# First mixer's probabilities transposed on VectorE and over DRAM instead of on TensorE

## The chip, the cores and the metric

The kernel runs on one core of a Trainium2 chip. The metric is the device time of one execution in microseconds (us). Engines are called by the profile's names: PE is TensorE (PEld its weight loads), DVE is VectorE, ACT is ScalarE, POOL is GpSimd, SP is SyncE. A name like L1737 is line 1737 of the kernel.

## The reference, cut to what matters

A decoder trunk of two layers on 512 tokens of width 1024. Layer 0 mixes tokens with three groups of dilated attention (16 heads of width 64), layer 1 with differential attention; each layer has a squared-ReLU MLP and a gated embedding behind the mixer. Only layer 0's mixer is changed:

```python
qkv = (h @ w_qkv).reshape(B, T, N_GROUPS_A, 3, HEADS_A, HEAD_DIM)
for g, (window, dilation) in enumerate(DIL_CONFIGS):      # (128,1), (512,4), (2048,16)
    o, l = dilated_group_attention(qkv[:, :, g, 0], qkv[:, :, g, 1], qkv[:, :, g, 2],
                                   window, dilation, rel_table)
    ...
alpha = softmax(stack(lses), axis=0)
o = sum(alpha[..., None] * stack(outs), axis=0)
return o.reshape(B, T, D_MODEL) @ w_o
```

Within a group: scores of queries against keys, plus a bias, a softmax over the keys, and the probabilities times the values. The last product contracts over the keys, and the scores have the queries on the partitions, so the probabilities are transposed in between.

## The kernel before

**Units.** Every weight matrix is cut into units of 1024x128. SP loads one (512 KB) into `w_raw` (L679), ACT rounds it to `w_hi` (`split_hi`, L884), DVE subtracts to get `w_lo` (`split_lo`, L1196), and PE multiplies in 24 matmuls of 512 columns (hi*hi, hi*lo, lo*hi; L1661 to L1663, or L1825 to L1827 where values are the rows). There are two buffers for each of these tiles. SP may issue the load of unit u once DVE has made `w_lo` of unit u-2.

**Steps and slots of the first mixer.** Heads go in pairs. Step s runs in nine slots, one unit each (the q, k, v projections of pair s), and beside them the attention of pair s-1. Steps 1 to 7 have both; step 8, the drain, has no projection and runs the first output units instead. On every engine `sub_a` writes out what slot i does, in the order of the program; for PE the attention's work of a slot stands ahead of the slot's unit. Odd steps make the far groups' values of two pairs in slots 0 to 3 (`values_unit`, evacuated together in slot 3); even steps have nine ordinary units.

**The attention of a pair** has four items (`ph` 0 and 1: the near group, 2 and 3: the two far groups), each a tile `probs[ph]` of 128x1024 in fp32:

- `scores_a` on PE into the bank `logits` (even items) or `turned` (odd items): items 0 and 1 in slot 0, items 2 and 3 in slot 2.
- Bias and row minimum on DVE (L1299, four instructions an item) and the exponential on ACT (L992), item i in slot i.
- The merge of the three groups' sums: `far_ps` on PE (L1848) and a chain of small DVE and ACT operations in slot 4, `near_ps` (L1857) in slot 6.
- `scale_a` on DVE (L1284, four instructions an item): items 2, 3, 0, 1 in slots 4, 5, 6, 7.
- `turn` on PE (L1737): 128x128 transposes of items 2 and 3 ahead of slot 6's unit (16 of them), of items 0 and 1 behind slot 8's unit (14), each bank copied back over `probs[ph]` half by ACT (L978, L1006) and half by DVE (L1305, L1368).
- `values_a` on PE (L1806) at the end of slot 8 into `attn`, which ACT and DVE split into the operand of the output projection (L1011, L1372).

SP's queue holds more than weights: `load_bias_a` in slot 3, `expand_a` in slot 6 (steps 1 to 6; ten DRAM to DRAM copies in small pieces that spread the next pair's bias, L711 and L715), and pieces of the second mixer's bias (L738) in slots 0, 4 and 8. SP counts its slots by the unit that it loads, some three slots ahead of PE. POOL does set-up and then waits for the first norm's sums (L866), behind the first mixer.

Of the kernel before, what the change touches and what calls it, by code (L numbers as in the profile page):

```python
# [65 lines left out]
A_SCORES = range(A_ITEMS)  # L66
A_MERGE = A_ITEMS
A_SCALES = {4: 2, 5: 3, 6: 0, 7: 1}
A_TURNS = {6: (2, 3), 8: (0, 1)}
A_NEAR = min(A_TURNS)  # L70
DRAIN_TURNS = {6: (2, 3), 7: (0, 1)}
DRAIN_SCALES = {4: (2,), 5: (3,), 6: (0, 1)}
A_TURN_ORDER = [ph for at_slot in sorted(A_TURNS) for ph in A_TURNS[at_slot]]
# [169 lines left out]
def build(nc, x, p, rel_bias, a_w_qkv, a_w_o, b_w_qkv, b_w_o, lq1, lk1, lq2, lk2, subln, norm_mix,  # L243
          norm_mlp, w_ff1, w_ff2, norm_ple, w_gate, w_proj, final_norm, selector, out):
    ctx = ExitStack()
    with ctx:
# [29 lines left out]
        probs_t = sb("probs_t", [P, T])  # L276
        ple_hi = [sb(f"ple_hi{i}", [P, KP, T], F32R) for i in range(2)]
# [64 lines left out]

        unit_out = [ps(f"unit_out{i}", [P, T]) for i in range(2)]
# [6 lines left out]
        near_in = attn[:, 0:2 * NT]  # L350
# [43 lines left out]
        def turns_at(has_proj, i):  # L394

            return (A_TURNS if has_proj else DRAIN_TURNS).get(i, ())

        def turns_behind(has_proj, i):

            return has_proj and i == A_UNITS - 1  # L400
# [181 lines left out]
        probs_ready = sem("probs_ready")  # L582
        turned_ready = sem("turned_ready")
# [233 lines left out]
        def _(pool):  # L817
# [43 lines left out]

            for norm in range(1, 7):
# [8 lines left out]
        def _(sc):  # L871
# [96 lines left out]
            def sub_a(s, par, i, has_proj, has_attn):  # L968
# [34 lines left out]
                if has_attn and turns_behind(has_proj, i):  # L1003
                    for ph in turns_at(has_proj, i):
                        wait(sc, turned_ready, (s - 1).times(A_ITEMS) + (A_TURN_ORDER.index(ph) + 1))
                        sc.activation(probs[ph][:, 0:T], a_bank(ph)[:, 0:T], ACT.Copy  # L1006
                                      ).then_inc(pt_a_ready, 1)
# [90 lines left out]
            def sub_b(s, par, i, has_proj, has_scores, has_prev, has_norm):  # L1098
# [6 lines left out]
                if has_prev:  # L1105
                    keys = b_width((i - 1) % B_ITEMS)
                    wait(sc, turned_ready, t)
# [81 lines left out]
        def _(ve):  # L1189
# [100 lines left out]
            def sub_a(s, par, i, has_proj, has_attn):  # L1290
                u = s.times(A_UNITS) + i
                start = s.reg is None and s.const == 0 and i == 0
                if has_attn and i in A_SCORES:
                    if i == 0:
                        wait(ve, bias_ready[1 - par], ((s - 1).half() + 1).times(16 * BIAS_LOADS))
                    wait_apart(ve, scores_ready, (s - 1).times(A_ITEMS) + (i + 1), (s_small, 16 * SMALL))
                    for cols, low_col, _ in a_segments(i):
                        to, of, by = probs[i][:, cols], a_bank(i)[:, cols], a_bias(1 - par, i, cols)
# [3 lines left out]
                if has_attn and not turns_behind(has_proj, i):  # L1302
                    for ph in turns_at(has_proj, i):
                        wait(ve, turned_ready, (s - 1).times(A_ITEMS) + (A_TURN_ORDER.index(ph) + 1))
# [11 lines left out]
                if has_attn and i == A_MERGE:  # L1316
# [14 lines left out]
                if has_attn and i == A_MERGE:  # L1331
# [17 lines left out]
                if has_attn and i == A_NEAR:  # L1349
# [783 lines left out]
```

## Time and profile before

| | |
|---|---|
| runs | 1615.31, 1614.57, 1614.43 us (median 1614.57) |
| profiled execution: span | 1614.3 us |
| PE busy | 1599.0 us (99%), 8244 matmuls |
| PEld, DVE, ACT, POOL busy | 82%, 56%, 38%, 4% |
| granted PE clock, mean | 0.998 |
| first mixer's steps 2 to 7 | 60.94 us each |
| DMA | 160.12 MB, mean 99 GB/s |

The profiled execution has no time of its own beside its span of 1614.3 us; the median of the runs lies 0.3 us above it, and that is taken for what lies around the span. A matmul's own duration in the profile is longer than the distance to the next one, since matmuls overlap: distances between starts say what PE work costs.

### The profile page before, as it was taken

The numbers are of one execution on the slowest core, as the hardware profiler recorded it, in microseconds if no ns is written. First come the engines' busy times: TensorE is split into PE (matmuls) and PEld (weight loads), VectorE is DVE, ScalarE is ACT, GpSimd is POOL, SyncE is SP. The second block draws the span as 40 slices with busy tenths as digits, with TensorE's granted clock in tenths as the row PEclk, the third lists the DMA queues.
The fourth block names the chain that finished last, engine by engine and source line by source line (L and its number), as shares of the span: only waits on it lengthen the run. The fifth ranks groups of instructions, "written<-read, shape, count | busy, mean of one in ns | idle before, by whom it ended". The sixth has DMA issues, their size and how long they took to land.

```text
span 1614.3 us, 22075 instructions
## 1 busy us (share of the span) xinstructions
PE 1599.0 (99%) x8244; PEld 1320.5 (82%) x8244; DVE 907.1 (56%) x1585; ACT 608.3 (38%) x1092; POOL 65.8 (4%) x68
## 2 busy tenths in 40 slices
PE   9999999999999999999999999999999999999998
PEld 7788888888888788888888878888878888888887
DVE  5365455555555863635455676777675363535565
ACT  5234334334334431222223444766652222222344
POOL 1000000000000200000001110000020000000111
PEclk9999999999999999999999999999999999999999
DMA  5633433443332333333333333323233333333331
GB/s 163 156 111 94 116 116 91 115 118 84 99 89 69 105 91 98 96 95 93 101 91 104 99 108 95 92 78 94 63 92 102 94 91 104 91 104 91 92 113 70
DMA packets 300571, 160.12 MB, mean 99 GB/s; under 512 B 31545, under 2 KB 295282, under 8 KB 300514
## 3 DMA queue, kind: packets, MB, share of 16 engines
q1 hardware_dynamic: 300112, 158.61, 34.6%
q0 software_dynamic: 144, 0.71, 0.2%
q8 instruction: 37, 0.61, 0.2%
q14 instruction: 20, 0.16, 0.0%
q10 hardware_dynamic: 258, 0.04, 0.0%
HBM read 157.11 MB, written 10.60 MB: 104 GB/s over the span
## 4 chain that ended last, share of the span: by engine, by line
PE 95%; POOL 1%; DMA 1%; DVE 1%; ACT 1%; issue 0%; SPq 0%; POOLq 0%; ACTq 0%; DVEq 0%
PE unit_out L1661 26%; PE unit_out L1663 26%; PE unit_out L1662 25%; PE turned L1737 2%; PE attn L1806 2%; POOL sumsq L866 1%; PE attn L2060 1%; PE unit_out L1825 1%; PE logits L1737 1%; DMA w_raw<-in_a_w_qkv_dram 1%; PE unit_out L1827 1%; PE unit_out L1826 1%; PE logits L1661 1%; PE misc L1737 1%; PE misc L1661 1%; PE misc L1663 1%
## 5 line engine op out<-in xcount | busy, mean ns | idle before, releaser
L1661 PE MATMUL unit_out<-act_hi,w_hi 128*128 128x512 f32 x1849 | 725.9, 393 | 3.0 <-DVE w_lo L1196 1.7
L1663 PE MATMUL unit_out<-act_hi,w_lo 128*128 128x512 f32 x1849 | 718.8, 389 | 0.0
L1662 PE MATMUL unit_out<-act_lo,w_hi 128*128 128x512 f32 x1849 | 718.0, 388 | 0.0
L884 ACT ACTIVATE w_hi<-w_raw 128x1024 fp32r<-128x1024 f32 (+3 forms) x256 | 271.0, 1058 | 461.2 <-PE unit_out L1663 349.4
L1661 PEld LDWEIGHTS unit_out<-act_hi,w_hi 128*128 128x128 f32 x1849 | 347.2, 188 | 78.2 <-DVE w_lo L1196 4.4
L1663 PEld LDWEIGHTS unit_out<-act_hi,w_lo 128*128 128x128 f32 x1849 | 347.1, 188 | 72.8
L1662 PEld LDWEIGHTS unit_out<-act_lo,w_hi 128*128 128x128 f32 x1849 | 347.4, 188 | 69.6 <-issue 0.2
L1196 DVE TENSOR_TENSOR w_lo<-w_raw,w_hi 128x1024 fp32r<-128x1024 f32 (+3 forms) x256 | 320.2, 1251 | 121.7 <-ACT w_hi L884 121.6
L1058 ACT ACTIVATE act_hi<-hidden 128x512 fp32r<-128x512 f32 x64 | 40.5, 633 | 243.4 <-DVE hidden L1459 243.4
L866 POOL TENSOR_TENSOR sumsq<-sumsq,square 128x512 f32<-128x512 f32 x41 | 57.8, 1410 | 1525.2 <-ACT square L912 1523.5
L1456 DVE TENSOR_TENSOR scaled<-unit_out,rstd 128x512 f32<-128x512 f32 x62 | 42.8, 690 | 67.8 <-PE unit_out L1663 67.7
L1275 DVE TENSOR_TENSOR h_a<-h_a,unit_out 128x512 f32<-128x512 f32 x39 | 26.8, 687 | 90.0 <-PE unit_out L1663 90.0
L1275 DVE TENSOR_TENSOR heads<-heads,unit_out 128x512 f32<-128x512 f32 x40 | 27.5, 686 | 84.2 <-PE unit_out L1663 84.2
L992 ACT ACTIVATE probs<-probs,w_raw 128x256 f32<-128x256 f32 (+1 forms) x128 | 61.8, 484 | 32.4 <-DVE w_raw L1299 32.4
L1462 DVE TENSOR_TENSOR act_lo<-hidden,act_hi 128x512 fp32r<-128x512 f32 x64 | 44.3, 692 | 44.7 <-ACT act_hi L1058 44.7
L1459 DVE SCALAR_TENSOR_TENSOR hidden<-scaled 128x512 f32<-128x512 f32 x64 | 44.3, 692 | 2.2
L1540 DVE CUSTOM_DVE_ANT_0 probs<-logits,bias 128x512 f32<-128x512 f32 (+3 forms) x64 | 28.2, 486 | 26.0 <-PE logits L1663 26.0
L1114 ACT ACTIVATE probs<-probs,low 128x512 f32<-128x512 f32 (+3 forms) x64 | 35.4, 554 | 7.4 <-DVE low L1540 7.4
L899 ACT ACTIVATE act_hi<-heads,gains 128x512 fp32r<-128x512 f32 x24 | 17.3, 722 | 49.1 <-DVE heads L1275 25.6
L1284 DVE TENSOR_SCALAR probs<-probs,w_raw 128x256 f32<-128x256 f32 (+1 forms) x128 | 35.2, 339 | 0.3
L1299 DVE CUSTOM_DVE_ANT_0 probs<-logits,bias 128x256 f32<-128x256 f32 (+1 forms) x64 | 21.1, 386 | 20.4 <-PE logits L1788 20.4
L1737 PE MATMUL turned<-ident,probs 128*128 128x128 f32 x208 | 30.5, 279 | 0.0
(295 smaller groups left out, 1390.9 us busy)
## 6 DMA issues: line engine op xcount, KB each, us to landing
w_raw<-in_w_ff_dram SPq DMA_DIRECT2D x128, 512.0 KB, 4.0
w_raw<-in_a_w_qkv_dram SPq DMA_DIRECT2D x56, 512.0 KB, 3.9
w_raw<-in_b_w_qkv_dram SPq DMA_DIRECT2D x24, 512.0 KB, 5.1
w_raw<-in_a_w_qkv_dram SPq DMA_DIRECT2D x32, 256.0 KB, 3.0
w_raw<-in_w_ple_gate_dram SPq DMA_DIRECT2D x16, 512.0 KB, 4.0
bias_tiles_b<-bias_vectors SPq DMA_DIRECT2D x16, 256.0 KB, 4.5
bias<-bias_tiles_b SPq DMA_DIRECT2D x8, 512.0 KB, 3.9
w_raw<-in_a_w_o_dram SPq DMA_DIRECT2D x8, 448.0 KB, 3.6
```

Source lines behind the costliest of these rows:

```text
L866: pool.tensor_tensor(sumsq[:, :], sumsq[:, :], square[n % 2][:, :], ALU.add).then_inc(sumsq_done, 1)
L884: sc.activation(weights_of(u)[0][:, 0:width, :], w_raw[par][:, 0:width, :], ACT.Copy).then_inc(hi_done, 1)
L992: e = sc.activation(probs[i][:, cols], probs[i][:, cols], ACT.Exp, bias=low_col, scale=-1.0, accum_out=sum_col)
L1196: ve.tensor_tensor(lo[:, 0:width, :], w_raw[par][:, 0:width, :], hi[:, 0:width, :], ALU.subtract).then_inc(lo_done, 1)
L1275: ve.tensor_tensor(h[:, n, :], h[:, n, :], unit_out[u.const % 2][:, :], ALU.add).then_inc(evac_done, 1)
L1456: ve.tensor_tensor(scaled[:, :], bank_of(u)[:, :], rstd[:, :], ALU.mult).then_inc(evac_done, 1)
L1459: ve.scalar_tensor_tensor(hidden[:, :], scaled[:, :], 0.0, scaled[:, :], ALU.max, ALU.mult).then_inc(hid_ready, 1)
L1462: ve.tensor_tensor(MID[layer][1][:, n, :], hidden[:, :], MID[layer][0][:, n, :], ALU.subtract).then_inc(hid_done, 1)
L1661: te.matmul(bank, w_k[0], hi, start=start, stop=False)
L1662: te.matmul(bank, w_k[0], lo, start=False, stop=False)
L1663: return te.matmul(bank, w_k[1], hi, start=False, stop=stop)
L1737: last = te.transpose(bank[:, dst:dst + P], src, ident[:, :])
```

## The change

In steps 1 to 7 PE transposes no probabilities any more. For each item:

1. DVE transposes the 32x32 blocks of `probs[ph]` into a new tile `blocks[:, ph, :]` (one instruction over 128x1024; slots 3, 4, 5, 6 for items 2, 3, 0, 1).
2. POOL's queue stores that tile to DRAM (512 KB), waits until it has landed, and loads it back into `probs[ph]` in four DMAs of 32 partitions (128 KB each, in runs of 1 KB), which puts the blocks in their places.
3. `values_a` waits for the four loads and reads `probs[ph]` in runs of 32 columns (`turned_order`).

In the same steps the scores of items 2 and 3 move from slot 2 to slot 1, additions and exponentials of items 0, 1 to slot 0 and of 2, 3 to slot 1, the merge from slots 4 and 6 to slots 2 and 4, scaling to slots 2 to 5; the near sums go through the bank `turned` instead of `attn`. The copies back (ACT and DVE) are gone in these steps. The drain keeps its slots, its transposes and its copies. `blocks` lies over `ple_hi`/`ple_lo`, which are filled after the mixer. The computation is the same.

```diff
-A_SCORES = range(A_ITEMS)
-A_MERGE = A_ITEMS
-A_SCALES = {4: 2, 5: 3, 6: 0, 7: 1}
-A_TURNS = {6: (2, 3), 8: (0, 1)}
-A_NEAR = min(A_TURNS)
+A_TURN_ORDER = (2, 3, 0, 1)
+
+A_SCORES = {0: (0, 1), 1: (2, 3)}
+A_SOFT = {0: (0, 1), 1: (2, 3)}
+A_SPREAD, A_MERGE, A_NEAR = 1, 2, 4
+A_SCALES = {2: (2,), 3: (3,), 4: (0,), 5: (1,)}
+A_BLOCKS = {3: (2,), 4: (3,), 5: (0,), 6: (1,)}
+
+DRAIN_SCORES = {0: (0, 1), 2: (2, 3)}
+DRAIN_SOFT = {n: (n,) for n in range(A_ITEMS)}
+DRAIN_SPREAD, DRAIN_MERGE, DRAIN_NEAR = 3, 4, 6
+DRAIN_SCALES = {4: (2,), 5: (3,), 6: (0, 1)}
 DRAIN_TURNS = {6: (2, 3), 7: (0, 1)}
...
+        with nc.sbuf_tensor("blocks", [P, A_ITEMS, 2 * T], F32) as blocks:
+            pass
...
+        blocks_d = nc.dram_tensor("turned_blocks", (A_ITEMS, P, 2 * T), F32, kind="Internal")
...
-        near_in = attn[:, 0:2 * NT]
...
+        def near_in(has_proj):
+
+            return (turned if has_proj else attn)[:, 0:2 * NT]
...
+        def blocks_at(has_proj, i):
+
+            return A_BLOCKS.get(i, ()) if has_proj else ()
...
+        def merge_slots(has_proj):
+
+            return (A_SPREAD, A_MERGE, A_NEAR) if has_proj else (DRAIN_SPREAD, DRAIN_MERGE, DRAIN_NEAR)
+
+        def turned_order(x):
+
+            return x.rearrange("p (i c) -> p i c", i=NT)
...
+            for n in range(A_ITEMS * (A_PAIRS - 1)):
+                ph = A_TURN_ORDER[n % A_ITEMS]
+                pool.wait_ge(blocks_ready, n + 1)
+                pool.dma_start(blocks_d.ap()[ph], blocks[:, ph, :]).then_inc(blocks_stored, 16)
+                pool.wait_ge(blocks_stored, 16 * (n + 1))
+                for j in range(NT):
+                    pool.dma_start(turned_order(probs[ph][j * SUB:(j + 1) * SUB, :]),
+                                   blocks_d.ap()[ph].rearrange("(i k) (j c) -> k j i c", i=NT, j=NT)[:, j]
+                                   ).then_inc(probs_landed[ph], 16)
...
@@ ScalarE, sub_a @@
-                if has_attn and not turns_behind(has_proj, i):
-                    for ph in turns_at(has_proj, i):
-                        wait(sc, turned_ready, (s - 1).times(A_ITEMS) + (A_TURN_ORDER.index(ph) + 1))
+                if has_attn:
+                    for ph in drain_turns_at(has_proj, i):
+                        wait(sc, turned_ready, A_TURN_ORDER.index(ph) + 1)
...
-                if has_attn and i in A_SCORES:
-                    wait(sc, logits_done, (s - 1).times(A_ITEMS) + (i + 1))
-                    for cols, low_col, sum_col in a_segments(i):
-                        e = sc.activation(probs[i][:, cols], probs[i][:, cols], ACT.Exp, bias=low_col,
+                for ph in soft_at(has_proj, i) if has_attn else ():
+                    wait(sc, logits_done, (s - 1).times(A_ITEMS) + (ph + 1))
+                    for cols, low_col, sum_col in a_segments(ph):
+                        e = sc.activation(probs[ph][:, cols], probs[ph][:, cols], ACT.Exp, bias=low_col,
                                           scale=-1.0, accum_out=sum_col)
...
@@ VectorE, sub_a @@
+                    for ph in blocks_at(has_proj, i):
+                        wait(ve, probs_ready, (s - 1).times(A_ITEMS) + (A_TURN_ORDER.index(ph) + 1))
+                        ve.transpose(out=blocks[:, ph, :].rearrange("p (j t q) -> p t j q", j=NT, q=SUB),
+                                     in_=probs[ph][:, :].rearrange("p (t j k) -> p t j k", j=NT, k=SUB)
+                                     ).then_inc(blocks_ready, 1)
-                if has_attn and i == A_MERGE - 1:
+                if has_attn and i == spread_at:
...
@@ TensorE @@
-            def values_a(par, ph):
+            def values_a(par, ph, landed):
 
 
                 for h, c, j, col in a_tiles(ph):
                     tile = 2 * (ph % 2) + h
                     out_rows = attn[j * E:(j + 1) * E, :]
+                    if landed:
+                        by = turned_order(probs[ph][:, :])[:, :, col // NT:(col + P) // NT]
+                    else:
+                        by = probs[ph][:, col:col + P].rearrange("p (r l) -> p r l", r=NT)
                     if ph < 2:
                         g, keys = 0, tile - 1 + c
                         to = by_residue(out_rows)[:, :, tile, :]
-                        by = probs[ph][:, col:col + P].rearrange("p (r l) -> p r l", r=NT)
                     else:
                         g, keys = c + 1, tile
-                        to, by = out_rows[:, tile * P:(tile + 1) * P], probs[ph][:, col:col + P]
+                        to = out_rows[:, tile * P:(tile + 1) * P].rearrange("p (i q) -> p i q", i=NT)
...
-                if has_attn and i == 0:
-                    wait(te, qk_ready, s.times(2))
-                    for ph in (0, 1):
-                        scores_a(par, ph).then_inc(scores_ready, 1)
-                if has_attn and i == 2:
-                    wait(te, evac_done, s.times(A_UNITS))
-                    for ph in (2, 3):
+                _, merge_at, near_at = merge_slots(has_proj)
+                for ph in scores_at(has_proj, i) if has_attn else ():
+                    if ph == 0:
+                        wait(te, qk_ready, s.times(2))
+                    if ph == 2:
+                        wait(te, evac_done, s.times(A_UNITS))
+                    if ph >= 2:
                         wait(te, logits_done, items + (ph - 1))
-                        scores_a(par, ph).then_inc(scores_ready, 1)
-                if has_attn and i == A_MERGE:
+                    scores_a(par, ph).then_inc(scores_ready, 1)
+                if has_attn and i == merge_at:
...
-                if has_attn and not turns_behind(has_proj, i):
-
-                    for ph in turns_at(has_proj, i):
+                if has_attn:
+
...
-                        wait(te, pt_a_ready, items + (n + 1))
-                        wait(te, pt_b_ready, items + (n + 1))
-                        last = values_a(par, ph)
+                        if has_proj:
+                            wait(te, probs_landed[ph], s.times(16 * NT))
+                        else:
+                            wait(te, pt_a_ready, n + 1)
+                            wait(te, pt_b_ready, n + 1)
+                        last = values_a(par, ph, has_proj)
```

## Rows read from the trace of the kernel before

**Rows 1.** The page, busy time and the chain that ended last

```profile
PE 1599.0 (99%) x8244; PEld 1320.5 (82%) x8244; DVE 907.1 (56%) x1585; ACT 608.3 (38%) x1092; POOL 65.8 (4%) x68
...
PE 95%; POOL 1%; DMA 1%; DVE 1%; ACT 1%; issue 0%; SPq 0%; POOLq 0%; ACTq 0%; DVEq 0%
```

**Rows 2.** Timeline of PE, end of step 3: start us, us, engine, line, operation [idle before <-releaser]

```profile
245.32 0.82 PE L1737 MATMUL logits<-ident,probs 128*128 128x128 f32 x6
...
246.95 3.25 PEld L1806 LDWEIGHTS attn<-probs,heads 128*64 128x64 f32 x60 [0.17 <-ACT probs L1006]
...
246.95 3.50 PE L1806 MATMUL attn<-probs,heads 128*64 128x128 f32 x60
...
250.37 0.33 PE L1781 MATMUL logits<-qk_hi 64*128 64x128 f32 x2
```

**Rows 3.** Timeline of PE, slots 4 and 6 of step 4

```profile
276.62 0.26 PE L1848 MATMUL logits<-w_raw,fold 128*32 128x16 f32 x8
...
276.80 0.50 PE L1661 MATMUL unit_out<-act_hi,w_hi 128*128 128x512 f32 x1
...
277.14 0.39 PE L1662 MATMUL unit_out<-act_lo,w_hi 128*128 128x512 f32 x1
...
287.91 0.25 PE L1857 MATMUL attn<-w_raw,fold 128*32 128x8 f32 x8
...
288.09 1.09 PE L1737 MATMUL logits<-ident,probs 128*128 128x128 f32 x8
...
289.81 0.47 PE L1661 MATMUL unit_out<-act_hi,w_hi 128*128 128x512 f32 x1
```

**Rows 4.** Windows: step 4, its us and busy us of each engine, PEclk, DMA share, GB/s

```profile
246.95:307.89 60.94, 60.94 (x384) 50.92 (x383) 33.10 (x84) 22.58 (x51) 0.00 (x0) 1.00 0.39 108
```

**Rows 5.** Timeline of DVE, step 4

```profile
271.28 0.69 DVE L1395 TENSOR_TENSOR scaled<-unit_out,rstd 128x512 f32<-128x512 f32 x1 [1.61 <-PE unit_out L1663]
...
273.40 1.22 DVE L1196 TENSOR_TENSOR w_lo<-w_raw,w_hi 128x1024 fp32r<-128x1024 f32 x1
...
279.93 1.13 DVE L1284 TENSOR_SCALAR probs<-probs,w_raw 128x256 f32<-128x256 f32 x4
```

**Rows 6.** Timelines of ACT, DVE and PE: slot 7's weights in steps 2, 4, 5

```profile
167.90 1.06 ACT L884 ACTIVATE w_hi<-w_raw 128x1024 fp32r<-128x1024 f32 x1 [6.14 <-DMA w_raw<-in_a_w_qkv_dram]
...
290.53 1.06 ACT L884 ACTIVATE w_hi<-w_raw 128x1024 fp32r<-128x1024 f32 x1 [6.89 <-DMA w_raw<-in_a_w_qkv_dram]
...
291.63 1.22 DVE L1196 TENSOR_TENSOR w_lo<-w_raw,w_hi 128x1024 fp32r<-128x1024 f32 x1 [0.84 <-ACT w_hi L884]
...
295.38 0.39 PE L1661 MATMUL unit_out<-act_hi,w_hi 128*128 128x512 f32 x1
...
350.21 1.06 ACT L884 ACTIVATE w_hi<-w_raw 128x1024 fp32r<-128x1024 f32 x1 [0.65 <-DMA w_raw<-in_a_w_qkv_dram]
```

**Rows 7.** Timeline of SP's queue ahead of those weights

```profile
275.06 2.50 SPq L711 DMA_DIRECT2D bias_tiles_a<-bias_vectors  x4
...
283.45 3.27 SPq L679 DMA_DIRECT2D w_raw<-in_a_w_qkv_dram  x2
```

**Rows 8.** DMA issues with KB each and us to landing, then POOL's timeline

```profile
w_raw<-in_a_w_qkv_dram SPq DMA_DIRECT2D x56, 512.0 KB, 3.9
...
out_dram<-heads SPq DMA_DIRECT2D x4, 512.0 KB, 3.0
...
qk_hi<-selector_dram POOLq DMA_DIRECT2D x1, 684.0 KB, 5.7
...
15.91 0.74 POOL L859 DMA_DIRECT2D qk_hi<-selector_dram  x1 [0.31 <-POOL table L856]
...
16.65 0.51 POOL L860 DMA_DIRECT2D qk_hi<-selector_dram  x1
```

**Rows 9.** Windows, step 4, slots 4 to 6, columns as above

```profile
277.00:283.00 6.00, 6.00 (x27) 4.96 (x27) 4.28 (x15) 1.42 (x3) 0.00 (x0) 1.00 0.34 89
...
283.00:290.00 7.00, 7.00 (x47) 5.85 (x47) 3.93 (x8) 0.64 (x1) 0.00 (x0) 1.00 0.58 137
```

More of the change, by code:

```diff
@@ L582, in build @@
         probs_ready = sem("probs_ready")
+        blocks_ready = sem("blocks_ready")
+        blocks_stored = sem("blocks_stored")
+        probs_landed = [sem(f"probs_landed{i}") for i in range(A_ITEMS)]
         turned_ready = sem("turned_ready")
@@ L1106, in sub_b @@
                     keys = b_width((i - 1) % B_ITEMS)
-                    wait(sc, turned_ready, t)
+                    wait(sc, turned_ready, t - (ITEMS_A - A_ITEMS))
                     sc.activation(probs_t[:, 0:keys], turned[:, 0:keys], ACT.Copy).then_inc(pt_a_ready, 1)
@@ L1315, in sub_a @@
                         ALU.mult).then_inc(spread_stat_ready, 1)
-                if has_attn and i == A_MERGE:
+                if has_attn and i == merge_at:
                     wait(ve, far_ps, s)
@@ L1330, in sub_a @@
                     next_lo(u)
-                if has_attn and i == A_MERGE:
+                if has_attn and i == merge_at:
                     wait(ve, shift_exp, s)
@@ L1348, in sub_a @@
                                      ALU.mult).then_inc(spread_share_ready, 1)
-                if has_attn and i == A_NEAR:
+                if has_attn and i == near_at:
                     wait(ve, near_ps, s)
-                    ve.tensor_copy(near_share[:, :], near_in[:, :]).then_inc(near_share_ready, 1)
+                    ve.tensor_copy(near_share[:, :], near_in(has_proj)).then_inc(near_share_ready, 1)
                     wait(ve, near_share_ready, s)
                 if has_attn:
-                    for ph in ((A_SCALES[i],) if i in A_SCALES else ()) if has_proj else DRAIN_SCALES.get(i, ()):
+                    for ph in scales_at(has_proj, i):
                         scale_a(s, ph)
@@ L1853, in sub_a @@
                     last.then_inc(far_ps, 1)
-                if has_attn and i == A_NEAR:
+                if has_attn and i == near_at:
                     wait(te, spread_share_ready, s)
@@ L1862, in sub_a @@
                     last.then_inc(near_ps, 1)
-                if has_attn and not turns_behind(has_proj, i):
-                    for ph in turns_at(has_proj, i):
+                if has_attn:
+                    for ph in drain_turns_at(has_proj, i):
                         n = A_TURN_ORDER.index(ph)
                         if n > 1:
-                            wait(te, pt_a_ready, items + (n - 1))
-                            wait(te, pt_b_ready, items + (n - 1))
+                            wait(te, pt_a_ready, n - 1)
+                            wait(te, pt_b_ready, n - 1)
                         wait(te, probs_ready, items + (n + 1))
@@ L1914, in sub_a @@
                                 for a in range(NT)]).then_inc(vt_ps, 1)
-                if has_attn and turns_behind(has_proj, i):
-                    for ph in turns_at(has_proj, i):
-                        n = A_TURN_ORDER.index(ph)
-                        if n > 1:
-                            wait(te, pt_a_ready, items + (n - 1))
-                            wait(te, pt_b_ready, items + (n - 1))
-                        wait(te, probs_ready, items + (n + 1))
-                        turn(a_bank(ph), [(col, probs[ph][:, col:col + P]) for _, _, _, col in a_tiles(ph)]
-                             ).then_inc(turned_ready, 1)
                 if has_attn and i == A_UNITS - 1:
                     for n, ph in enumerate(A_TURN_ORDER):
-                        wait(te, pt_a_ready, items + (n + 1))
-                        wait(te, pt_b_ready, items + (n + 1))
-                        last = values_a(par, ph)
+                        if has_proj:
[4 more added lines that the diff above has]
+                        last = values_a(par, ph, has_proj)
                     last.then_inc(pv_done, 1)
@@ L2055, in sub_b @@
                         wait(te, v_ready, s + A_PAIRS)
-                    wait(te, pt_a_ready, t)
+                    wait(te, pt_a_ready, t - (ITEMS_A - A_ITEMS))
                     if has_norm and i == 1:
```

43 lines of the change are left out of this document (19 added, 24 removed).

## The prediction

> **What bounds the kernel now.** I read the page first: PE is busy for 1599.0 of 1614.3 us, and the chain that ended last is PE for 95% [rows 1]. Then the windows, step by step: each of steps 2 to 7 takes 60.94 us, with PE busy in all of it, DVE for 33.10 and ACT for 22.58 [rows 4]. So in the first mixer only two things move the end: PE work that goes, and anything that comes too late for PE. The distances between PE's starts say what work costs: 24 matmuls of a unit lie 0.227 us apart, a slot is 5.44 us, and nine slots leave about 12 us of a step for the attention's own PE work.
>
> **What goes.** Behind slot 8's unit, 14 transposes start at 245.32 and the value products at 246.95, the last 0.17 us of it a wait for ACT's copy [rows 2]. Ahead of slot 6's unit, 16 transposes start at 288.09 and the unit at 289.81 [rows 3]. That is 1.63 + 1.72 = 3.35 us a step, the wait included, and 7 steps make 23.45 us. The drain's 30 transposes stay. The mean durations in the page (0.28 us) would give more than twice that, but they overlap; the starts decide. The copies that go with them were on ACT and DVE, which had time: they count nothing.
>
> **What moves on PE.** A small fp32 group between two units costs more than its matmuls: the far sums start at 276.62, their unit at 276.80, and that unit's second matmul comes 0.34 us later where 0.23 is usual [rows 3]; with some 0.09 at the entry I take 0.2 us for each additional place where PE changes over. Even steps have as many such places after as before (the transposes of V now join the far sums instead of the scores of items 2 and 3). In odd steps V's transposes stood with the near sums and stand alone now: 4 x 0.2 = 0.8 us. The value products read `probs` in four runs of 32 columns instead of one of 128. No row has that form; their 60 matmuls take 3.42 us [rows 2], and I take no change (a tenth more would be 0.34 a step, 2.4 us in all, and I see no reason for less). PE's sum: 23.45 - 0.8 = 22.65 us less.
>
> **What DVE gets.** The transpose of 128x1024 has no row. Nearest is the subtraction over 128x1024, 1.22 us [rows 5]; below, one column a cycle as in the scaling (four of 128x256 in 1.13) [rows 5] is about the same; above I allow double, 2.4. I take 1.2. Four of them, 4.9 us a step, replace four copies of 0.69. DVE stays at some 35 of 58 us, so what counts is the order inside a slot, since `w_lo` of the next unit stands behind the new work. Slot 0 has two items' additions ahead of it instead of one, and four of them with their sums' spread take 1.43 us (271.97 to 273.40) [rows 5]. Value products end and scores start at 250.37 [rows 2]; DVE first needs ACT's split of `attn`, its own half and an evacuation, 2.1 us together, then 2.8 for two items and 1.2 for `w_lo`, which ends at 256.5. PE wants it after 1.6 us of scores and a unit of 5.44, at 257.4: 0.9 us to spare. Slot 1: PE first makes the scores of items 2 and 3, some 2 us, so everything behind has as much more time. Slot 2 is the fullest (evacuation 0.69, merge chain about 1.6, `w_lo` 1.22, scaling 1.13, a split 0.69: 5.4 us of a slot of 5.44 plus V's transposes), but only its evacuation slips, by a few tenths, and PE wants that bank a whole slot later. Slot 3: the transpose of item 2 follows the evacuation of slot 2's unit, which ends at 271.97 [rows 5], so the block is ready at 273.2, and `w_lo` follows at the place it has now (273.40), since the additions of item 3 left it. Cost of all this: 0; if the transpose took 2.4 us, slot 3 would still keep about 0.9 us.
>
> **What POOL and the DMAs get.** For each item POOL issues a store, waits until it lands, and issues four loads. No such chain is in the trace. POOL's two issues took 0.74 and 0.51 us; a 512 KB store from SP landed after 3.0 us, POOL's 684 KB load in the crowded start after 5.7 [rows 8]. An item so takes between 3.0 + 4 x 0.51 = 5.0 and 5.7 + 4 x 0.74 = 8.7 us; I take 4.4 + 4 x 0.63 = 6.9. The items queue behind each other, since POOL waits: the last load of item 1 is issued at 273.2 + 4 x 6.9 = 300.8 and landed by 2.4 us later, 303.2. PE wants it for the last 16 of 60 value matmuls: values start 3.35 us earlier than now, at 304.54, plus 44/60 x 3.42 = 2.5 gives 307.05 in step 4. So 3.8 us are left, and none below an item time of 7.9 us. Odd steps do not evacuate in slots 0 to 2, so their blocks come earlier. After 7.9 each further us costs 4 us a step, 28 in all.
> The Trainium skill (DMA: Bandwidth & Descriptors, section on the anatomy of a SWDGE DMA) gives a POOL-issued DMA 2.0 us plus bytes over 436 GB/s. By it, as an estimate, the store would take 3.2 us and the item some 5.7, and no wait would come up.
>
> **Weights of slot 7.** This is the place where a step that shrinks meets something that doesn't. SP stands in `expand_a` from 275.06 and issues slot 7's load only at 283.45 [rows 7]; it lands about 7.0 us later, where the median is 3.9 [rows 8], and ACT sat 6.89 us idle until 290.53 for it. DVE ends `w_lo` at 292.85 and PE starts the unit at 295.38 [rows 6]: 2.53 us to spare. SP's start hangs on slot 3's `w_lo`, which does not move, but slot 6 loses 1.72 us, so 0.8 us is left in steps 4 and 6. In step 2 ACT starts at 167.90 for a unit at 173.50 (295.38 less two steps) [rows 4, 6]: 3.28 - 1.72 = 1.6. In odd steps the weights are there at 350.21 for a unit at 356.32, ACT and DVE need 2.3 us: 3.8 - 1.72 = 2.1. The new traffic, 1 MB an item, falls just there: DMA engines are busy for 34 and 58% in these windows without it [rows 9]. Its delay d on this load lies between 0 and another full 7.0 us; one more 512 KB piece in front at the median is 3.9. I take 2.2 us, since the engines are half free and the pieces of the two queues alternate. Waits: 2 x 1.4 + 0.6 + 3 x 0.1 = 3.7 us (step 7 has no `expand_a`). With d = 3.9 it is 2 x 3.1 + 2.3 + 3 x 1.8 = 13.9; with 0, nothing. Behind a late slot 7 the loads of POOL get the same time more, so the two waits don't add.
>
> **Sum.** 1614.3 - 22.65 + 3.7 = 1595.35 for a profiled execution, and 0.3 more against the median: 1595.6 us.
>
> **Rivals.**
> *No wait anywhere.* The DMA engines' free half takes the traffic, d stays below 0.8. For it: PE is never short of weights now. Against it: 4 MB more in a step that moved 108 GB/s x 60.94 us = 6.6 MB [rows 4]. Time: 1614.3 - 22.65 + 0.3 = 1592.0.
> *POOL's chain decides, and the kernel gets slower.* Above 7.9 us an item, PE waits at the end of slot 8; from 7.9 + 22.65/28 = 8.7 us on nothing is gained, which is the top of the sum from rows. What would push it over is DVE holding up POOL: if each of the five issues had to wait for the DVE instruction under way, that is on average 33.10/60.94 x 1.22/2 = 0.33 us, 1.7 us an item. From 6.9 this makes 8.6, a wait of 273.2 + 34.4 + 2.4 - 307.05 = 2.95 a step, and 1612.6; from 8.7 it makes 10.4, 10.2 us a step, and 1663. Against it: POOL's two issues of 0.74 and 0.51 us stood in a stretch in which DVE worked too [rows 8].
> The Trainium skill (SBUF — State Buffer, section on the two separate sides of SBUF) has this as a rule: in a two-port mode, DVE locks POOL out of writing descriptors. The scaling's 0.28 us for 256 columns is one column a cycle, so this kernel's fp32 instructions look free of that mode; whether the transpose is, no row shows.
> *Weights far later.* d of 5.4 us eats all (6 x 5.4 less the spare 0.8 + 0.8 + 1.6 + 6.3 = 22.9): no change, 1614.6. The load would have to take 12.4 us instead of 7.0.
> *DVE's first slots.* If slot 0's `w_lo` were 1 us late in seven steps, 1602. I count 0.9 us of room, so the count would have to be off by twice that.
>
> **How the numbers follow.** Measurement tells some 0.2% (3.2 us) from no change. Forecast (waits of 1 to 10 us in all): 0.52, 1593 to 1602. No wait: 0.20, 1591 to 1593. POOL's chain: 0.08 with part of the gain left (1602 to 1611), 0.03 level, 0.08 slower. Weights far later: 0.03 level, 0.01 slower. DVE's slots: 0.05, 1599 to 1606. Faster 0.85, level 0.06, slower 0.09. The range goes from 1591 (all PE work gone and nothing lost) to 1606, which leaves out some 0.17, mainly POOL's upper cases. Its bottom is firm, because only PE work is taken away.
>
> **What would show it.** Steps of 57.5 us where nothing waits; 57.6 plus what slot 7 waits in steps 2, 4 and 6. PE idle ahead of L1661 released by `w_lo` in slot 7, about 1 us each. Value products right behind slot 8's unit, with no idle time released by a DMA on `probs`. POOL's items about 7 us apart with issues of 0.5 to 0.75. A DVE transpose of about 1.2. Slot 7's load landing after some 9 us. The prediction is wrong if POOL's items take over 8 us, if the value matmuls lie further apart than 0.057 us, or if the unit's own cadence of 0.227 changes.

## The result and the profile after

The changed kernel takes 1636.43 us (median of 4 runs, 1631.47 to 1637.76) against 1614.5 us (1614.37 to 1615.31): a ratio of 1.0129, 95% interval 1.0115 to 1.0143. It is slower by 1.3%; forecast were 1595.6 us and a range of 1591 to 1606. The execution of 1631.47 us had a mean granted PE clock of 0.992, the three others 0.986.

The page of the changed kernel, busy time, the chain that ended last, and PE's costliest group (busy us, mean ns | idle before it, and what ended most of it):

```profile
PE 1590.2 (97%) x8034; PEld 1305.4 (80%) x8034; DVE 919.4 (56%) x1585; ACT 591.5 (36%) x1064; POOL 143.2 (9%) x208
...
PE 87%; DMA 5%; SPq 2%; DVE 2%; POOL 1%; ACT 1%; issue 1%; ACTq 0%; POOLq 0%; DVEq 0%
...
L1704 PE MATMUL unit_out<-act_hi,w_hi 128*128 128x512 f32 x1849 | 732.1, 396 | 32.2 <-DVE w_lo L1238 30.7
```

PE has 210 matmuls fewer, as meant, but its busy time fell by only 8.8 us [rows 1], since some of the others now run at half clock (below), and PE now idles 30.7 us for `w_lo`. The chain that ended last, nearly all PE before, runs 5% over DMA and 2% over SP's queue. L1704 is L1661 of before, L1238 is L1196.

The windows of the changed kernel show where: step 4, then three stretches in it, then step 7 (columns as in [rows 4]: the window, its us and the busy us of PE, PEld, DVE, ACT, POOL, then PEclk, DMA share, GB/s).

```profile
258.45:324.34 65.89, 59.97 (x353) 48.98 (x352) 34.63 (x84) 20.06 (x47) 10.98 (x20) 0.95 0.60 163
...
305.30:311.20 5.90, 0.04 (x1) 0.00 (x0) 1.22 (x2) 1.06 (x1) 2.73 (x5) 0.78 1.12 302
...
311.30:315.20 3.90, 3.90 (x9) 3.10 (x10) 1.73 (x2) 1.03 (x1) 0.43 (x1) 0.50 0.92 315
...
316.00:320.00 4.00, 4.00 (x19) 3.26 (x19) 0.69 (x1) 0.99 (x2) 0.95 (x2) 1.00 0.87 230
...
454.70:512.44 57.74, 57.74 (x353) 47.53 (x352) 33.61 (x82) 18.93 (x45) 10.95 (x20) 1.00 0.55 161
```

A step is counted from the first value product of one step to the next step's. Step 7 takes 57.74 us, close to the 57.5 to 57.6 of the forecast. Step 4 takes 65.89 against 60.94 [rows 4], and steps 2 to 6 take 67.22, 64.81, 65.89, 64.32 and 66.04. They differ from step 7 in two stretches. First PE does nothing for 5.9 us while the DMA engines are full. Then its granted clock is 0.50, that is 1.2 GHz, and 9 matmuls are in work in 3.90 us, 0.43 us from start to start; at full clock it is 19 in 4.00 us, 0.23 us apart.

What PE waits for can be followed back through the timelines. SP's queue in step 4, the answer to [rows 7]; the last lines are the end of `expand_a` and slot 7's load:

```profile
286.60 3.09 SPq L747 DMA_DIRECT2D bias_tiles_a<-bias_vectors  x4
289.74 0.57 SPq L751 DMA_DIRECT2D bias_tiles_a<-bias_vectors  x1
290.35 7.74 SPq L747 DMA_DIRECT2D bias_tiles_a<-bias_vectors  x4
298.13 0.60 SPq L751 DMA_DIRECT2D bias_tiles_a<-bias_vectors  x1
298.78 5.27 SPq L715 DMA_DIRECT2D w_raw<-in_a_w_qkv_dram  x2
```

ACT, DVE and PE behind that load, the answer to [rows 6]:

```profile
308.89 1.06 ACT L930 ACTIVATE w_hi<-w_raw 128x1024 fp32r<-128x1024 f32 x1 [13.34 <-DMA w_raw<-in_a_w_qkv_dram]
...
309.98 1.23 DVE L1238 TENSOR_TENSOR w_lo<-w_raw,w_hi 128x1024 fp32r<-128x1024 f32 x1 [8.20 <-ACT w_hi L930]
...
311.26 0.79 PE L1704 MATMUL unit_out<-act_hi,w_hi 128*128 128x512 f32 x1 [5.92 <-DVE w_lo L1238]
```

And POOL's queue beside it:

```profile
285.35 0.56 POOL L901 DMA_DIRECT2D turned_blocks<-blocks  x1 [34.66 <-DVE blocks L1352]
...
289.19 2.18 POOL L904 DMA_DIRECT2D probs<-turned_blocks  x4 [3.29 <-DMA turned_blocks<-blocks]
291.37 0.56 POOL L901 DMA_DIRECT2D turned_blocks<-blocks  x1
...
300.23 0.56 POOL L901 DMA_DIRECT2D turned_blocks<-blocks  x1
...
309.07 0.56 POOL L901 DMA_DIRECT2D turned_blocks<-blocks  x1
...
314.77 2.18 POOL L904 DMA_DIRECT2D probs<-turned_blocks  x4 [5.14 <-DMA turned_blocks<-blocks]
```

The window from the load's issue to ACT's start:

```profile
298.78:308.89 10.11, 6.56 (x29) 5.08 (x28) 1.84 (x2) 0.00 (x0) 4.00 (x8) 0.99 1.01 242
```

The reader sees two delays, one behind the other. SP's ten copies of `expand_a` took 286.60 to 298.73, 12.1 us, where they took 8.4 (275.06 to 283.45 [rows 7]); they start at the same place of the step (28.1 us into it), and the load was issued 3.8 us later in it. Then it took 10.1 us to ACT's start instead of 7.1, with the DMA engines full (1.01). Both stretches lie beside POOL's items, which start 6.0, 8.9 and 8.8 us apart. In the other steps it is the same: the copies take 11.2 to 12.6 us in steps 1 to 6, against 7.7 to 8.4 before.

The six waits ahead of slot 7's unit, in steps 1 to 6, are 3.98, 6.37, 3.92, 5.92, 3.87 and 6.67 us, 30.73 in all. The five steps 2 to 6 take 328.28 us instead of 5 x 57.72 = 288.6: 39.7 more, 26.75 of it waits. The other 12.9 are the slow clock: behind these five waits PE works for 3.0 to 6.1 us at a clock of 0.50 and loses about half of that; beyond their waits the steps are 1.7 to 3.2 us longer, 2.6 in the mean. Behind step 1's wait the clock falls too, and ten matmul distances take 3.98 us instead of 2.27, 1.7 us more:

```profile
113.70:117.60 3.90, 3.90 (x10) 3.08 (x11) 2.38 (x3) 1.06 (x1) 0.00 (x0) 0.56 0.92 282
```

From the forecast's 1614.3 - 22.65 the account is 1591.65 + 30.73 + 12.9 + 1.7 = 1637.0, and the span is 1635.8.

At the end of slot 8 nothing waits, as PE's timeline shows where the unit ends and the value products start:

```profile
324.02 0.39 PE L1706 MATMUL unit_out<-act_hi,w_lo 128*128 128x512 f32 x1
324.34 3.50 PE L1852 MATMUL attn<-probs,heads 128*64 128x128 f32 x60
```

Around the span lie 2.0 us (the profiled execution took 1637.76 us), and 1.9 or 2.0 in all later runs. The 0.3 of the forecast set the span of one execution, 1614.3, against the median of others; in later executions the kernel before has spans of 1611.8 to 1613.6. So the profiled one was the longer by about 1.7 us, and by luck this cancels the rest of the 2.0. Executions of one kernel or of kernels with equal steps differ by some 2 us outside these steps, which covers the 1.2 us of the account, so step lengths and waits say more than single totals.

### The profile page after: what moved, and what is told of

The parts are those of the page before. It is cut to its first block, busy times and chain, and to the rows that moved or that the text cites. A ratio compares the mean times of both kernels' runs of the same rounds, so it can differ in the third digit from the quotient of the medians.

```text
span 1635.8 us, 21746 instructions
## 1 busy us (share of the span) xinstructions
PE 1590.2 (97%) x8034; PEld 1305.4 (80%) x8034; DVE 919.4 (56%) x1585; ACT 591.5 (36%) x1064; POOL 143.2 (9%) x208
## 4 chain that ended last, share of the span: by engine, by line
PE 87%; DMA 5%; SPq 2%; DVE 2%; POOL 1%; ACT 1%; issue 1%; ACTq 0%; POOLq 0%; DVEq 0%
PE unit_out L1704 24%; PE unit_out L1705 23%; PE unit_out L1706 23%; DMA w_raw<-in_a_w_qkv_dram 5%; SPq L747 2%; PE attn L1852 2%; POOL sumsq L912 1%; DVE w_lo L1238 1%; PE attn L2100 1%; PE turned L1780 1%; PE unit_out L1871 1%; PE unit_out L1872 1%; PE unit_out L1873 1%; PE logits L1704 1%; ACT w_hi L930 1%
## 5 line engine op out<-in xcount | busy, mean ns | idle before, releaser
L1704 PE MATMUL unit_out<-act_hi,w_hi 128*128 128x512 f32 x1849 | 732.1, 396 | 32.2 <-DVE w_lo L1238 30.7
L1704 PEld LDWEIGHTS unit_out<-act_hi,w_hi 128*128 128x128 f32 x1849 | 350.6, 190 | 111.4 <-DVE w_lo L1238 36.8
L1238 DVE TENSOR_TENSOR w_lo<-w_raw,w_hi 128x1024 fp32r<-128x1024 f32 (+3 forms) x256 | 319.7, 1249 | 146.2 <-ACT w_hi L930 145.9
L904 POOL DMA_DIRECT2D probs<-turned_blocks x112 | 61.3, 554 | 135.3 <-DMA turned_blocks<-blocks 133.0
L901 POOL DMA_DIRECT2D turned_blocks<-blocks x28 | 15.7, 560 | 276.7 <-DVE blocks L1352 276.7
```

Of the source, the lines that this page charges most:

```text
L904: pool.dma_start(turned_order(probs[ph][j * SUB:(j + 1) * SUB, :]), blocks_d.ap()[ph].rearrange("(i k) (j c) -> k j i c", i=NT, j=NT)[:, j ...
L1238: ve.tensor_tensor(lo[:, 0:width, :], w_raw[par][:, 0:width, :], hi[:, 0:width, :], ALU.subtract).then_inc(lo_done, 1)
L1704: te.matmul(bank, w_k[0], hi, start=start, stop=False)
```

## The experiments

Each kernel ran on one chip beside the kernel before; ratios with an interval are of three rounds, times without one are of a single execution. "After" is the changed kernel.

**No bytes.** After, with POOL's DMAs cut to four columns: every issue, wait and DVE transpose stays, and nearly no bytes move. The probabilities are not put in place.

```diff
-pool.dma_start(blocks_d.ap()[ph], blocks[:, ph, :])
+pool.dma_start(blocks_d.ap()[ph][:, 0:4], blocks[:, ph, 0:4])
...
-pool.dma_start(turned_order(probs[ph][j * SUB:(j + 1) * SUB, :]), blocks_d.ap()[ph].rearrange(...)[:, j])
+pool.dma_start(probs[ph][j * SUB:(j + 1) * SUB, 0:4], blocks_d.ap()[ph][j * SUB:(j + 1) * SUB, 0:4])
```

> The changed kernel with POOL's queue issuing the same 28 stores and 112 loads, each cut to 4 columns (16 bytes a partition), so that items 0 to 3 are not put in place; everything else as it is. Theory (the bytes of the round trip delay slot 7's weights): the six waits of PE ahead of slot 7's unit (3.9 to 6.7 us) are gone, every step takes the 57.7 us of step 7, span 1592 (1590 to 1595). Rival (the moved slots on DVE and ACT, or POOL's waits, make the delay): waits stay, 1625 to 1636.

It took 1593.58 us, span 1591.6. SP's queue in step 4 and the window of step 5 of this kernel:

```profile
265.60 2.77 SPq L747 DMA_DIRECT2D bias_tiles_a<-bias_vectors  x4
...
273.02 0.62 SPq L751 DMA_DIRECT2D bias_tiles_a<-bias_vectors  x1
273.68 3.53 SPq L715 DMA_DIRECT2D w_raw<-in_a_w_qkv_dram  x2
```

```profile
295.15:352.89 57.74, 57.74 (x354) 47.52 (x353) 33.75 (x82) 19.14 (x45) 10.17 (x20) 1.00 0.41 114
```

`expand_a` is back to 8.0 us of issues, ACT starts on the load 7.2 us behind its issue, no step waits, the clock stays at 1.00, and steps 2 to 7 take 57.70 to 57.77 us. The whole loss is the bytes' doing, and PE's and DVE's part of the forecast is right.

**Spread `expand_a`.** After, with the ten copies sent one or two at a time behind the loads of slots 4 to 8 and 0, instead of all ten behind slot 6's:

```diff
-if u == 8 or u > A_UNITS and u % A_UNITS == 6 and u // A_UNITS < A_PAIRS - 1:
-    expand_a(u // A_UNITS + 1)
+for at_slot, pieces in [(4, (0, 1)), (5, (2, 3)), (6, (4,)), (7, (5, 6)), (8, (7, 8)), (9, (9,))]:
+    pair = (u - at_slot) // A_UNITS + 1
+    if (u - at_slot) % A_UNITS == 0 and 1 < pair < A_PAIRS:
+        for n in pieces:
+            expand_piece(pair, n)
```

> The changed kernel with the ten copies of expand_a issued two at a time behind the weight loads of slots 4 to 8 and 0, not all in one piece ahead of slot 7's load. Theory (half of the delay is SP standing in expand_a, whose ten issues take 12.1 us instead of 8.4, and half is its pieces queued in front of the load): slot 7's waits fall from 5.1 us in the mean to under 1, and the halved clock behind them goes too; 1593 to 1600. Rival (the DMA engines are simply full in slots 4 to 7): the wait only changes its place, 1612 to 1636. Third possibility: POOL's items, 8.9 us each, now come too late for the value products, 1 to 3 us a step, 1598 to 1612.

It took 1602.73 us, ratio 0.9924 (0.9907 to 0.994). The waits of slot 7 are gone, with all of POOL's bytes still there. Steps take 58.6 to 60.8 us, because now PE waits up to 2.78 us for the last item's loads; the timeline of PE in step 2 of this kernel:

```profile
185.72 1.09 PE L1863 MATMUL attn<-probs,heads 128*64 128x128 f32 x16 [2.78 <-DMA probs<-turned_blocks]
```

So the block of ten copies is what turned the traffic into late weights, and behind that wait stands the rival of POOL's chain, with items 5.8 to 9.5 us apart and one in step 6 10.9, with 2.31 us of pause between its loads for which the profile names no wait. At 1602.73 us it is the third possibility, not the theory's 1593 to 1600.

**Traffic in the kernel before.** The kernel before (PE transposes and all) with the same store and loads over a tile that nothing uses, each item started when that item's scaling is done, and POOL waiting for the landing:

```diff
...
+pool.wait_ge(probs_ready, n + 1)
+pool.dma_start(extra_d.ap()[ph], extra[:, ph, :]).then_inc(extra_stored, 16)
+pool.wait_ge(extra_stored, 16 * (n + 1))
+for j in range(NT): pool.dma_start(extra[...], extra_d...).then_inc(extra_landed, 16)
+pool.wait_ge(extra_landed, 16 * NT * (n + 1))
```

> The kernel before, with its PE transposes, and the same 28 stores and 112 loads of POOL's queue added, over a tile of their own that nothing uses. Theory (bytes alone delay the load by some 6 to 7 us): with 2.5 us to spare in even steps and 3.8 in odd ones PE waits some 4.7 and 2.2 us, 21 us in six steps, and half clock behind each adds some 2 us, so 1640 to 1650. Rival (the delay needs the shorter step): 1614 to 1622.

It took 1616.46 us; steps stay at 60.94, two are 61.4 and 61.5. The forecast number was missed, and the trace says why the test was no fair one: here only one item starts beside `expand_a`, at its end, and the others come behind slot 7's load. In step 4 the ten copies take 8.6 us, about as in the kernel before, and the load 9.7 us to ACT's start instead of 7.1: one item's loads beside it cost about the 2.53 us that PE had to spare. Hence the next.

**Traffic in place.** The same, with the items started at the place of the step where after has them (behind `w_lo` of slots 3 to 6):

```diff
-pool.wait_ge(probs_ready, n + 1)
+pool.wait_ge(lo_done, A_UNITS * (n // A_ITEMS + 1) + n % A_ITEMS + 5)
...
```

> The kernel before, with its PE transposes, and POOL's stores and loads over an unused tile, now started behind the weights' subtraction of slots 3, 4, 5 and 6, where the changed kernel has them; the earlier run had three of the four items behind expand_a. Theory (bytes beside expand_a and the load make slot 7's weights late by 6 to 7 us, whatever PE does): PE waits some 4 us in even and 2 us in odd steps, with half clock behind it, 1630 to 1648. Rival (the shorter step is needed as well): 1614 to 1620.

It took 1652.36 us. The timelines of SP, ACT and PE in step 4 of this kernel, then its windows, step 4 and 4 us behind the wait:

```profile
303.73 5.08 SPq L685 DMA_DIRECT2D w_raw<-in_a_w_qkv_dram  x2
...
315.22 1.06 ACT L908 ACTIVATE w_hi<-w_raw 128x1024 fp32r<-128x1024 f32 x1 [14.09 <-DMA w_raw<-in_a_w_qkv_dram]
...
317.59 0.79 PE L1685 MATMUL unit_out<-act_hi,w_hi 128*128 128x512 f32 x1 [4.56 <-DVE w_lo L1220]
```

```profile
264.44:332.91 68.47, 63.91 (x383) 52.75 (x383) 32.96 (x84) 22.57 (x51) 10.92 (x20) 0.95 0.56 157
...
317.60:321.60 4.00, 4.00 (x10) 3.13 (x11) 3.80 (x11) 1.06 (x1) 2.01 (x4) 0.50 0.84 207
```

The copies take 10.0 to 11.2 us. The six waits are 2.87 to 4.56 us and make 21.6, steps 2 to 6 take 65.9 to 68.5 us, and step 7 stays at 60.94. The kernel before, with nothing taken from PE, gets late weights and half clock behind all six waits. So the traffic at that place is enough by itself; the waits are shorter than in after (30.73 us) in the main because PE here has its 1.72 us more to spare.

**Half the bytes.** After, with whole stores and loads of four columns (the probabilities are not put in place).

```diff
-pool.dma_start(turned_order(probs[ph][j * SUB:(j + 1) * SUB, :]), blocks_d.ap()[ph].rearrange(...)[:, j])
+pool.dma_start(probs[ph][j * SUB:(j + 1) * SUB, 0:4], blocks_d.ap()[ph][j * SUB:(j + 1) * SUB, 0:4])
```

> The changed kernel with whole stores and loads cut to 4 columns, so that the probabilities are not put in place. If bytes decide, whichever way they go, half of them leave about half of the delay: waits of 1 to 3 us, 1600 to 1615. If the loads' 1 KB runs are what hurts: no wait, 1592 to 1595. If the stores hurt: 1625 to 1636.

1604.69 us. Odd steps take 57.73 us; even steps wait 2.54, 2.04 and 1.92 us and take 61.5 to 62.2, with the slow clock behind. With the waits' spare times of the forecast (1.6, 0.8, 0.8) the load is 4.1, 2.8 and 2.7 us late, against 8.0, 6.7 and 7.5 with all bytes. Most of it lies in the copies, which take 10.4 to 10.9 us in even steps and 8.4 to 8.8 in odd ones; in even steps ACT starts 7.8 to 8.0 us behind the load's issue.

**A wait filled.** After, with 32 idle transposes on PE ahead of slot 7's unit in steps 1 to 6, so that PE is busy instead of waiting:

```diff
+if has_proj and has_attn and i == 7 and not (s.reg is None and s.const == A_PAIRS - 1):
+    for _ in range(32):
+        te.transpose(turned[:, 0:P], ident[:, :], ident[:, :])
```

> The changed kernel with 32 idle transposes on PE (3.6 us) ahead of slot 7's unit in steps 1 to 6, in the time in which PE waits anyway. Theory (the clock is halved because PE stood still, and that costs some 2.2 us behind each wait): granted clock 1.0 behind the wait, 10 to 13 us less than the changed kernel, 1623 to 1627. Rival (the clock falls for another reason): 1634 to 1638.

1627.59 us. Odd steps, where the transposes fill the wait, fall from 64.81 and 64.32 to 61.94 and 61.85 us: the slow clock's price is 2.9 and 2.5 us. In even steps 3.11, 2.15 and 2.36 us of waiting are left; the clock falls behind the first two and stays at 1.00 behind the third. Slot 7's unit starts 52.6 us into step 4 against 52.8 in after: the weights come hardly earlier, only what PE does meanwhile is different.

**A longer wait filled.** The same with 60 in even steps, compared with the wait filled by 32.

```diff
-for _ in range(32):
+for _ in range(32 if par else 60):
```

> The changed kernel with 32 idle transposes ahead of slot 7's unit in odd steps, as before, and 60 (6.8 us) in even ones, where 32 left 2 to 3 us of standing still and the clock at half behind it. Theory (standing still lowers the clock, from 2 to 3 us of it on): all six waits are filled, no stretch at 0.5, even steps of 64 to 65 us, 1620 to 1624 in all. Rival (the load on DMA or the length of the wait as such lowers it): even steps stay at 66 to 67, 1626 to 1630.

1637.49 us, so the total missed the expectation. Filled even steps do take 64.3 us, with a clock of 1.00 through the late weights. But two gaps are new, of 3.93 and 3.84 us, at the start of steps 3 and 5, where the loop over two steps jumps back; with 32 in every step there were none. PE's timeline and the windows of this kernel:

```profile
195.30 0.47 PE L1824 MATMUL logits<-qk_hi 64*128 64x128 f32 x2 [3.93 <-issue]
```

```profile
170.00:190.00 20.00, 20.00 (x150) 17.70 (x149) 5.57 (x6) 3.70 (x4) 4.91 (x9) 1.00 0.83 251
...
196.00:200.00 4.00, 4.00 (x24) 3.42 (x25) 2.87 (x17) 1.62 (x7) 0.00 (x0) 0.50 0.00 0
```

The first window has DMA engines 83% busy and a full clock, the second has no DMA at all and half the clock, right behind an idle PE. So the slow clock follows PE's idleness, not the traffic (in which idle stretches it falls is another question, below). Where the two gaps come from wasn't tried; the profile names no wait.

**Slots alone.** After, with the probabilities transposed on PE again (items 2, 3 ahead of slot 6's unit, items 0, 1 ahead of slot 8's, where before they stand behind it) and without the round trip, so that only the moved scores, merge and scaling are left of the change.

```diff
-return A_BLOCKS.get(i, ()) if has_proj else ()
+return ()
...
-return () if has_proj else DRAIN_TURNS.get(i, ())
+return ({6: (2, 3), 8: (0, 1)} if has_proj else DRAIN_TURNS).get(i, ())
```

> The moved slots alone: scores, softmax, merge and scaling where the changed kernel has them, but PE transposes items 2 and 3 ahead of slot 6's unit and 0 and 1 ahead of slot 8's, with the copies back; no blocks, no round trip. Theory (the moved slots cost PE only the additional changeover in odd steps and save the wait for the copies): 1614 to 1616. Rival (they crowd DVE so that weights come late): 1620 or more.

1615.24 us, ratio 1.0004 (0.9994 to 1.0013); steps take 61.03 to 61.05 us against 60.94. The moved slots cost 0.1 us a step, the wait of 0.17 us for ACT's copy [rows 2] being gone here.

**Spread in the kernel before.** The kernel before with the spread `expand_a`.

```diff
-if u == 8 or u > A_UNITS and u % A_UNITS == 6 and u // A_UNITS < A_PAIRS - 1:
-    expand_a(u // A_UNITS + 1)
+for at_slot, pieces in [(4, (0, 1)), (5, (2, 3)), (6, (4,)), (7, (5, 6)), (8, (7, 8)), (9, (9,))]:
+    ...
+    expand_piece(pair, n)
```

> The kernel before with expand_a spread over the slots and nothing else. Theory: its PE waits for no weights in steps 1 to 7, so spreading gains nothing there, 1612 to 1615; the gain of the spread and pipelined version is the change's own. Rival: the spread alone is worth something, under 1611.

1614.45 us beside 1614.15; steps 60.94 each. The block's late weights were covered there, so spreading gains nothing by itself.

**Spread, and POOL's store ahead.** The spread version with POOL issuing the next item's store before it waits for this item's, so that a store runs beside the loads:

```diff
+def store(n):
+    ph = A_TURN_ORDER[n % A_ITEMS]
+    pool.wait_ge(blocks_ready, n + 1)
+    pool.dma_start(blocks_d.ap()[ph], blocks[:, ph, :]).then_inc(blocks_stored[n % 2], 16)
 for n in range(A_ITEMS * (A_PAIRS - 1)):
     ph = A_TURN_ORDER[n % A_ITEMS]
-    pool.wait_ge(blocks_ready, n + 1)
-    pool.dma_start(blocks_d.ap()[ph], blocks[:, ph, :]).then_inc(blocks_stored, 16)
-    pool.wait_ge(blocks_stored, 16 * (n + 1))
+    if n % A_ITEMS == 0:
+        store(n)
+    if n % A_ITEMS < A_ITEMS - 1:
+        store(n + 1)
+    pool.wait_ge(blocks_stored[n % 2], 16 * (n // 2 + 1))
```

> The changed kernel with expand_a spread as before over the slots, and POOL issuing the store of the next item ahead of the loads of this one, so that it waits for no landing with an item ready. Theory (what is left in the spread version, 1.2 to 2.8 us of PE waiting for the last item's loads, comes of POOL's serial items of up to 9 us): the waits at the value products go, steps of 57.7 to 58.2, 1594 to 1597. Rival (the DMA engines' bytes are the limit, so that stores and loads side by side take as much longer): 1600 to 1604 as the spread version.

1592.28 us (1591.75 to 1592.43), ratio 0.9863 (0.9846 to 0.9879). The windows of steps 4 and 5 of this kernel, and of 8 us in step 4:

```profile
235.59:293.29 57.70, 57.70 (x353) 47.62 (x352) 33.84 (x83) 20.07 (x47) 11.18 (x20) 1.00 0.68 185
293.29:351.03 57.74, 57.74 (x354) 47.53 (x353) 34.52 (x84) 19.14 (x45) 11.15 (x20) 1.00 0.66 184
...
275.03:283.20 8.17, 8.17 (x37) 6.76 (x37) 4.24 (x7) 1.06 (x1) 4.31 (x8) 1.00 1.01 294
```

DMA engines are busier than in after (0.68 against 0.60), for 8 us as full as beside after's late load (1.01), and nothing waits: the whole of the forecast's gross gain is there. Full engines alone did not make PE wait here; with the block in one piece they do (next). This version beats both kernels.

**POOL's store ahead alone.** After with that order on POOL and `expand_a` in one piece.

> The changed kernel with POOL's queue pipelined (next item's store ahead of this item's loads) and expand_a in one piece where it is. Theory (slot 7's weights are late because of expand_a ahead of their load together with the bytes; POOL's order only matters for the value products): slot 7's waits stay between 3 and 8 us, 1625 to 1645. Rival (a better POOL order alone removes the crowding): under 1605.

1648.8 us, slower than after and above the 1645 expected at most: the waits ahead of slot 7's unit are 5.68, 9.15, 8.71, 9.14, 4.01 and 7.01 us. Packing POOL's bytes tighter beside the block makes the weights later still. The same edit loses 12 us here and gains 10 behind the spread.

**`expand_a` behind slot 8's load.** After, with the block whole but two units later.

```diff
-u % A_UNITS == 6
+u % A_UNITS == 8
```

> The changed kernel with expand_a in one piece, but issued behind slot 8's load and not behind slot 6's; the next load is that of the next step's slot 0. Theory (what hurts is that a load which PE needs soon stands behind expand_a): slot 7's waits are gone; slot 0's unit has 9.6 us to spare in the kernel before where slot 7's has 2.5; what remains is POOL's late last item, so 1595 to 1606. Rival (the wait moves to slot 0 or 1): 1610 to 1636.

1606.84 us, just above the 1606 expected at most. The waits of slot 7 are gone; waits of 3.84, 1.90 and 0.70 us for the last item's loads came, and three of 0.49 to 0.99 for `w_lo`. The windows around the longest, the wait and what follows:

```profile
181.00:186.00 5.00, 1.16 (x16) 0.92 (x14) 1.12 (x1) 1.57 (x2) 0.00 (x0) 0.77 0.70 190
186.00:195.00 9.00, 9.00 (x52) 7.45 (x49) 5.62 (x21) 5.49 (x18) 0.00 (x0) 0.56 0.25 79
```

Moving the block is worth most of what spreading it is; the step with the longest wait still takes 65.76 us, since half clock follows it.

## Why the prediction was wrong

- **PE's sum** (22.65 us less) was right: in the runs that have no waits, steps 2 to 7 are 3.2 us shorter each, 22.5 in seven if step 1 is like them. Its parts were less so: with 3.35 us less in even steps and 3.15 in odd ones taken, no bytes gives 3.24 and 3.17 to 3.21, so the four changeovers more cost next to nothing and something of 0.1 us a step, as in slots alone, was not in the sum.
- **Value products** in runs of 32 columns: no change, right (60 in 3.50 us, as in [rows 2]).
- **DVE** was right. The profile's group of the transposes (min/median/max in ns):

```profile
L1352 DVE STREAM_TRANSPOSE blocks<-probs x28: 1233/1235/1247, 85.6 to 496.4; 128x1024 f32<-128x1024 f32 x28
```

  Taken were 1.2 us. The first slots cost 0.1 us a step at most.
- **POOL's item** was taken at 6.9 us. In step 7, without `expand_a`, the items take 5.4 to 6.3; beside the block up to 9.0, and one in step 6 11.3 with the pause of 2.31 us named above, both over the bound of 8.7. The 2.4 us to the landing of the last load had no row; a 128 KB load took 4.1 in the median. The wait expected from 7.9 on did not come in after, because the late slot 7 gave the loads the same time more, as the forecast said of the two waits (argued, from the end of slot 8 above). In the spread version, without that cover, it came: up to 2.78 us a step.
- **Weights of slot 7** is the step that failed. The place, the order of the waits and the mechanism were right; the size of d was not. "Its delay d on this load lies between 0 and another full 7.0 us ... I take 2.2 us, since the engines are half free and the pieces of the two queues alternate." With the spare times of the forecast, d was 8.0, 6.7 and 7.5 us in even steps and about 6.0 in odd ones. The waits are 30.73 us, not 3.7. Two things were missing in it. The forecast let the traffic delay only the load itself, which in step 4 took 3.0 us longer; but SP's ten copies ahead of it are slowed too, by 3.7 us, and the load stands behind them in the queue. And "half free" was the mean of a window before the new traffic (0.58 [rows 9]); with it the engines are full while the load is under way (1.01).
- **The slow clock** had no term, and no reason was given for leaving it out. It adds 14.6 us in six steps. With the right waits and no such term the forecast would still have said 1591.65 + 30.73 + 0.3 = 1622.7 us.
- **The rival "weights far later"** had the sum right up to its threshold (all gain eaten from d = 5.4 us); this is the one that came true, and it got 4 chances in 100, one of them for slower. Taking the middle of d's bounds, 3.5, would have given 2 x 2.7 + 1.9 + 3 x 1.4 = 11.5 us of waits. The choice leaned on the mean load of DMA engines in windows that the new traffic had not yet entered.

The Trainium skill (DMA: Bandwidth & Descriptors, section on issuing engines not being separate queues) says that DMAs from SP, ACT and GpSimd run on the same 16 engines and interleave there. The trace agrees: 8.0 us of SP issues and no wait with POOL's bytes gone, 12.1 us and a load of 10.1 us with them (7.2 without). By the Trainium skill (DMA: Bandwidth & Descriptors, section on the anatomy of a SWDGE DMA) a DMA issued by POOL takes 2.0 us plus bytes over 436 GB/s, for a 512 KB store an estimate of 3.2 us. The median here was 5.4, and the measurement decides.

What stays open: why SP's issues themselves get longer, behind which waits the clock falls, the two gaps named above, and POOL's pause in step 6.

## What to carry to other kernels

When a change adds DMA traffic, look at what else is issued in the same stretch, not at the mean load: a block of small copies in front of a load on one queue delays that load twice, once by longer issues and once by a slower transfer. Before giving up such a change, spread the block and overlap the new chain; here that turned 1.3% slower into 1.4% faster, while the second edit alone made it worse. And give a PE wait more than its own length: a wait of 3.9 to 6.7 us cost another 1.7 to 3.2 us here by the clock behind it.

## What the runs showed of the hardware

- PE's granted clock was 0.50 (1.2 GHz) for 3.0 to 6.1 us of its work behind all six waits of after, 3.87 to 6.67 us long. It fell too behind waits of 1.90 (`expand_a` behind slot 8's load), 1.92, 2.04 and 2.54 (half the bytes) and 2.15 us (a wait filled), but stayed at 1.00 behind 2.36 us (a wait filled) and 2.78 us (spread). So these runs give no simple rule by the wait's length. DMA load alone, at 251 and 294 GB/s, left it at 1.00.
- SP's time to issue ten copies of small pieces rose from 8.4 to 12.1 us (step 4) when POOL's queue moved 512 KB stores and loads beside it; with the stores' bytes alone it was 10.5.
- POOL issues a 128-partition store in 0.56 us, and four loads of 32 partitions in 2.18, next to DVE transposes of 1.23 us. Issues with a DVE instruction beside them all the time took 0.555 us in the median, those with none 0.552: nothing shows DVE holding up the issue, the price that the forecast's rival needed.
- A DVE transpose of 32x32 blocks over 128x1024 in fp32 takes 1.235 us, the same as a subtraction of that size.
